# Reordering the start of a hybrid pool and state-space block: a tile's squares ahead of the step sizes, their exponential in two pieces, and one set of transposes ahead of the first product

## The chip, the cores and the metric

The kernel runs on one core of a Trainium2 chip. The metric is device time in microseconds (us) of one execution; lower is better. The core's engines each work through a stream of instructions of their own, in order, and wait for one another through semaphores: TensorE (PE, with its weight loads as PEld), VectorE (DVE), ScalarE (ACT), GpSimd (POOL), and SyncE (SP), which here only issues DMAs.

## The reference, cut to what matters

One decoder layer on x of 1024 tokens by 1024 channels, float32. What the change touches is the front of it:

```python
mod = jax.nn.silu(c) @ w_ada + b_ada
shift, scale, gate = jnp.split(mod, 3, axis=-1)
h = rmsnorm(x, norm_pre) * (1.0 + scale[:, None, :]) + shift[:, None, :]
proj = h @ w_in            # 6144 columns: u_pool, z_pool, u_ssm, z_ssm, g_pool, g_ssm
...
dt = jnp.exp(log_dt)[:, None]          # step sizes of the states
abar = exp(lam * dt)                   # used by the state-space mixer much later
```

`rmsnorm(x, gain)` is `x * rsqrt(mean(x*x) + 1e-6) * gain`, per token. Behind it come two mixers, gates and three more square products, and the output `x + gate * rmsnorm(out, norm_post)`.

## The kernel before, in words

Every engine's order is written out by hand; there is no scheduler. All products are split in three: an operand is written as a high part and a low part (`split_hi` or `h_high` on ScalarE, `split_lo` or `split_h` on VectorE), and TensorE adds high by high, high by low and low by high.

x is read as eight tiles of 128 tokens (`x_tok`), in order, with the constants (which hold the identity) between tiles 2 and 3. The sum of squares of each tile goes to one of two engines (`X_TILES_ACT`, `X_TILES_DVE`): ScalarE squares tiles 0, 1, 3 for the first half and 4, 6, 7 for the second, VectorE tile 2 and tile 5 (`square_sum`, L1404). For each half VectorE waits for all four sums, forms the variance (L1417), ScalarE takes the root (L1032), VectorE makes the reciprocal (`newton`) and four diagonal matrices (`diag`, L1422). TensorE multiplies 128 by 128 blocks of x by such a diagonal (`transposed(k, tiles)`, L1976), which transposes and normalises them at once. K tiles 0 to 3 are done half by half, in the order 2, 0, 1, 3 (`XT_ORDER`); K tiles 4 to 7 afterwards, whole. Only four PSUM areas hold them, so a transposed tile must be copied out before its area is written again: `xt_out(k)` on ScalarE copies K tile k to `h_full` and counts `xt_taken`. `transposed(4)` waits for one such copy, that of K tile 2; `transposed(5)` for two, so for K tile 3 as well, whose area it takes. K tiles 0 and 1 have no copy of their own: `h_of(0)` and `h_of(1)` read them in PSUM.

The modulation: ScalarE applies SiLU to c, and for each K tile k VectorE sums rows of `w_ada` against it (`scale_sum`, `shift_sum`, L1400) to give one column each of `g_col` and `s_col` (L1436, L1438). `h_of(k)` on ScalarE (L1051) then makes K tile k of h, `h_high(k)` (L1057) its high part and `split_h(k)` on VectorE (L1442) its low part, which counts `h_done`. In VectorE's order `split_h(0)` stands between `scale_sum(1)` and `shift_sum(1)`, and `split_h(1)` behind `shift_sum(2)`.

TensorE runs the first two products (`gs` 0 and 1) side by side, one K tile of each in turn: `step(n, k)` waits for `h_done` above k. `step(1, 0)` also waits for `h_of(1)`, whose PSUM area it takes, and for the low part of its weights. The third product is fitted in as K tiles come; from the fourth on whole products follow.

On VectorE the step sizes of the states come first of all: `plain_angles` computes `dt = exp(log_dt)` and two multiples of the angle on 128 by 64 values, a chain of small instructions, each of which waits for the one before. Their result is next read after the last `split_h`, by `reduced_angles`.

Of the kernel before, what the change touches and what calls it, by code (L numbers as in the profile page):

```python
# [36 lines left out]
CH = 8  # L37
NC = SEQ // CH
HALF = 512
G = 64  # L40
# [83 lines left out]
def previous(p):  # L124

    if p == 4:
        return JOB[USES[0]]
    q = p - 2
    while q >= 0 and USES[q][0] == "ga":
        q -= 2  # L130
    return None if q < 0 else JOB[USES[q]]


def half_pi_parts():

    unit = 10 ** 35
    rest, parts = 157079632679489661923132169163975144, []
    rest <<= 34
    for bits in (10, 22, 34):
        n = rest // (unit << (34 - bits))  # L140
        parts.append(n / 2 ** bits)
        rest -= n * (unit << (34 - bits))
    return parts + [rest / (unit << 34)]


class Steps:
# [13 lines left out]
    def do(self, ins):  # L160
        self.did(ins)
        self.landed()


def build(nc, x, c_d, cols_d, consts_d, a_re_d, a_im_d, log_dt_d, bc_d, w_ada_d, wstream_d, pool_d, w_out_d, out):
    ctx = ExitStack()
    with ctx:
        def sem(name):
            return ctx.enter_context(nc.semaphore(name))
# [44 lines left out]
        def hb(q, k):  # L214

            return bop[:, 2 * (k // 4):2 * (k // 4) + 2, q, k % 4, :]

        def halves(ap):

            return ap.rearrange("p (f m) -> p f m", f=2)  # L220
# [171 lines left out]
        v_sums, par_in, xt_taken = sem("v_sums"), sem("par_in"), sem("xt_taken")  # L392
# [54 lines left out]
        def slot(u):  # L447

            return SLOT[JOB[u]]
# [21 lines left out]
        par = {}  # L471
# [5 lines left out]
        wide = {}  # L477
# [47 lines left out]
        def rounded(steps, out_, in_, scale):  # L525

            steps.do(nc.vector.tensor_scalar(out_, in_, scale, MAGIC, ALU.mult, ALU.add))
            steps.do(nc.vector.tensor_scalar(out_, out_, MAGIC, None, ALU.subtract))

        def exp(steps, out_, in_, width):  # L530

            do = steps.do
            tt, stt, ts = nc.vector.tensor_tensor, nc.vector.scalar_tensor_tensor, nc.vector.tensor_scalar
            k, r, p, q = (wide[z][:, 0:width] for z in ("k", "r", "p", "q"))
            do(ts(q, in_, -87.0, 88.0, ALU.max, ALU.min))
            rounded(steps, k, q, 1.4426950408889634)
            do(stt(r, k, -0.693359375, q, ALU.mult, ALU.add))
            do(stt(r, k, 2.12194440054690583e-4, r, ALU.mult, ALU.add))
            c = [1.0, 1 / 2, 1 / 6, 1 / 24, 1 / 120, 1 / 720]
            do(ts(p, r, 1 / 5040, None, ALU.mult))  # L540
            for a in reversed(c):
                do(stt(p, p, a, r, ALU.add, ALU.mult))
            do(ts(p, p, 1.0, None, ALU.add))
            do(ts(bits[:, 0:width], k, 127.0, 8388608.0, ALU.add, ALU.mult))
            do(tt(p, p, bits[:, 0:width].bitcast(F32), ALU.mult))
            do(stt(out_, in_, -87.0, p, ALU.is_ge, ALU.mult))

        def plain_angles(steps):

            do, tt, ts = steps.do, nc.vector.tensor_tensor, nc.vector.tensor_scalar  # L550
            exp(steps, par["dt"], par["ldt"], G)
            do(tt(wide["ang"][:, 0:G], par["aim"], par["dt"], ALU.mult))
            do(ts(wide["ang"][:, G:], wide["ang"][:, 0:G], float(CH), None, ALU.mult))

# [9 lines left out]
        def reduced_angles(steps):  # L564

            do, stt = steps.do, nc.vector.scalar_tensor_tensor
            k, r, q = (wide[m] for m in ("k", "r", "q"))
            src = wide["ang"]
            for scale in (2048.0, 1.0):
                rounded(steps, k, src, 1.0 / (1.5707963267948966 * scale))  # L570
                for part in half_pi_parts():
                    do(stt(r, k, -part * scale, src, ALU.mult, ALU.add))
                    src = r
            rounded(steps, q, k, 0.25)
            do(stt(q, q, -4.0, k, ALU.mult, ALU.add))
# [430 lines left out]
        def _(act):  # L1006
            fn = nc.scalar.activation

            def split_hi(p):

                act.wait_ge(raw_in[p % 2], 16 * (p // 2) + 16)
                if p != 2 and previous(p) is not None:
                    act.wait_ge(mm_done, previous(p) + 1)
                fn((wx_hi if p == 2 else w_hi[p % 2])[:, :, :], raw[p % 2][:, :, :], ACT.Copy).then_inc(hi_done, 1)  # L1014
# [22 lines left out]
            def xt_out(k):  # L1037

                act.wait_ge(xt_done, XT_ORDER.index(k) + 1)
                fn(h_full[k][:, :], xt[k][:, :], ACT.Copy).then_inc(xt_taken, 1)  # L1040
# [13 lines left out]
            def h_high(k):  # L1054

                act.wait_ge(h_ready, k + 1)
                fn(hb(0, k), halves(h_full[k][:, :]), ACT.Copy).then_inc(h_hi_done, 1)  # L1057

            split_hi(0)
            xt_out(2)  # L1060
            h_of(0)
            h_high(0)
            xt_out(3)
            split_hi(1)
            h_of(1)
            xt_out(4)
# [319 lines left out]
        def _(dve):  # L1386
            tt, stt = nc.vector.tensor_tensor, nc.vector.scalar_tensor_tensor
            ts = nc.vector.tensor_scalar
            steps = Steps(dve, dve_step)
            do, did = steps.do, steps.did  # L1390

            def split_lo(p):

                dve.wait_ge(hi_done, SPLIT[USES[p]] + 1)
                hi, lo = (wx_hi, wx_lo) if p == 2 else (w_hi[p % 2], w_lo[p % 2])
                tt(lo[:, :, :], raw[p % 2][:, :, :], hi[:, :, :].bitcast(F32), ALU.subtract).then_inc(raw_free[p % 2], 1)  # L1396
# [5 lines left out]
            def square_sum(t):  # L1402
                dve.wait_ge(tile_in[t], 16)
                stt(rt[1][:, :], x_tok[:, t, :], 1.0, x_tok[:, t, :], ALU.mult, ALU.mult,  # L1404
                    accum_out=stat[:, 0, t:t + 1]).then_inc(v_sums, 1)

            dve.wait_ge(par_in, 16 * 3)
            plain_angles(steps)
            for half_ in range(2):
                cols4 = slice(4 * half_, 4 * half_ + 4)  # L1410
                for t in X_TILES_DVE[half_]:
                    if half_:
                        dve.wait_ge(v_sums, half_)
                    square_sum(t)
                dve.wait_ge(v_sums, half_ + 1)
                dve.wait_ge(x_sums, 3 * half_ + 3)
                ts(stat[:, 1, cols4], stat[:, 0, cols4], 1.0 / D, EPS, ALU.mult, ALU.add).then_inc(x_var, 1)  # L1417
                dve.wait_ge(x_root, half_ + 1)
                newton(steps, cols4, 1.0)
                dve.wait_ge(small_in, 16)  # L1420
                for t in range(4 * half_, 4 * half_ + 4):
                    ts(diag[:, t, :], ident, stat[:, 4, t:t + 1], None, ALU.mult).then_inc(x_scaled, 1)  # L1422
                if half_ == 0:
                    dve.wait_ge(cols_in, 16)
                    do(ts(g_col[:, :], b_ada[:, KT:2 * KT], 1.0, None, ALU.add))
# [14 lines left out]
            def split_h(k):  # L1440
                dve.wait_ge(h_hi_done, k + 1)
                tt(hb(1, k), halves(h_full[k][:, :]), hb(0, k).bitcast(F32), ALU.subtract).then_inc(h_done, 1)  # L1442

            dve.wait_ge(silu_ready, 1)
            for k in range(KT):
# [8 lines left out]
                if k == 3:  # L1454
                    split_lo(2)
            split_h(KT - 1)
            reduced_angles(steps)
            sine(steps)
            split_lo(3)
# [445 lines left out]
            for t in range(CH):  # L1905
# [3 lines left out]
                bank, g, r = ps[slot(u)], gt[t % 2], rt[t % 2]  # L1909
# [24 lines left out]
        def _(pe):  # L1934
# [34 lines left out]
            def transposed(k, tiles):  # L1969

                if k >= 4:
                    pe.wait_ge(xt_taken, 5 if k == 7 else k - 3)
                for t in tiles:
                    if k == XT_ORDER[0]:
                        pe.wait_ge(x_scaled, t + 1)
                    last = mm(xt[k][:, t * P:t * P + P], x_tok[:, t, k * P:k * P + P], diag[:, t, :],  # L1976
                              start=True, stop=True)
                if CH - 1 in tiles:
                    last.then_inc(xt_done, 1)

            def step(n, k):

                u = ("gs", n)
                if k == 0:
                    begin(u)
                    if n == 1:
                        pe.wait_ge(h_ready, 2)
                    elif n == 2:
                        pe.wait_ge(xt_taken, 4)
                pe.wait_ge(h_done, k + 1)  # L1990
                last = k_step(u, k, *h)
                if k == KT - 1:
                    last.then_inc(mm_done, 1)

            for tiles in (range(0, 4), range(4, CH)):
                for k in XT_ORDER[:4]:
                    transposed(k, tiles)
            transposed(4, range(CH))
            step(0, 0)
            transposed(5, range(CH))  # L2000
            step(1, 0)
            third = {2: (0, 1), 3: (2,), 5: (3,), 7: (4, 5, 6, 7)}
            for k in range(1, KT):
# [278 lines left out]
```

## Time and profile before

| what | value |
|---|---|
| time, median of 3 runs | 953.89 us (953.86 to 953.91) |
| profiled execution, first to last instruction (span) | 951.7 us |
| PE busy | 930.3 us, 98% of the span |
| DVE busy | 640.0 us, 67% |
| ACT busy | 347.6 us, 37% |
| mean granted TensorE clock | 0.999 of full speed |

The profiled execution's own time stands nowhere apart from the three runs; its span lies 2.2 us below their median, which is what lies around the first and last instruction. PE busy counts matmuls whose ends are modelled, so a busy PE is not PE at its peak. Idle time is worth something only where the chain that ends last passes through it.

### The profile page before, as it was taken

The numbers are of one execution on the slowest core, as the hardware profiler recorded it, in microseconds if no ns is written. First come the engines' busy times: TensorE is split into PE (matmuls) and PEld (weight loads), VectorE is DVE, ScalarE is ACT, GpSimd is POOL, SyncE is SP. The second block draws the span as 40 slices with busy tenths as digits, with TensorE's granted clock in tenths as the row PEclk, the third lists the DMA queues.
The fourth block names the chain that finished last, engine by engine and source line by source line (L and its number), as shares of the span: only waits on it lengthen the run. The fifth ranks groups of instructions, "written<-read, shape, count | busy, mean of one in ns | idle before, by whom it ended". The sixth has DMA issues, their size and how long they took to land.

```text
span 951.7 us, 11609 instructions
## 1 busy us (share of the span) xinstructions
PE 930.3 (98%) x4408; PEld 781.6 (82%) x4408; DVE 640.0 (67%) x916; ACT 347.6 (37%) x453; POOL 45.4 (5%) x82
## 2 busy tenths in 40 slices
PE   4999999999999999999999999999999999999997
PEld 4888888888888888888888888888888888888885
DVE  5988999877788887437898789665344444455232
ACT  6741353334444444434444436441022221223111
POOL 0019700000000000000000000000000000000000
PEclk9999999999999999999999999999999999999999
DMA  9843355446555444556898582597643268422222
GB/s 352 299 153 125 124 200 166 156 159 195 174 188 202 147 176 152 191 131 183 228 245 224 132 205 88 165 339 262 182 161 107 89 228 202 144 89 89 89 88 89
DMA packets 95719, 164.60 MB, mean 173 GB/s; under 512 B 38576, under 2 KB 55088, under 8 KB 95664
## 3 DMA queue, kind: packets, MB, share of 16 engines
q1 hardware_dynamic: 85872, 159.31, 52.1%
q10 hardware_dynamic: 9792, 4.56, 1.9%
q8 instruction: 35, 0.57, 0.3%
q14 instruction: 20, 0.16, 0.1%
HBM read 116.64 MB, written 47.19 MB: 172 GB/s over the span
## 4 chain that ended last, share of the span: by engine, by line
PE 97%; DVE 1%; ACT 1%; DMA 1%; issue 0%; ACTq 0%; DVEq 0%
PE ps L1948 49%; PE ps L2068 20%; PE ps L2190 9%; PE psb L2068 8%; PE ps L2139 2%; PE psb L2119 2%; PE psb L2128 2%; PE psa L2107 2%; PE psa L2026 1%; PE psa L1948 1%; DMA par_are<-in_a_re 1%; PE psb L2026 0%; PE psb L1976 0%; ACT gt L1028 0%; DVE mod_out L1400 0%
## 5 line engine op out<-in xcount | busy, mean ns | idle before, releaser
L1948 PE MATMUL ps<-bop,w_hi 128*128 128x512 f32 x1120 | 300.6, 390 | 0.9 <-DVE bop L1442 0.9
L1948 PEld LDWEIGHTS ps<-bop,w_hi 128*128 128x128 f32 x1120 | 209.3, 188 | 44.0 <-issue 1.1
L1948 PE MATMUL ps<-bop,w_lo 128*128 128x512 f32 x560 | 172.3, 389 | 0.0
L1948 PEld LDWEIGHTS ps<-bop,w_lo 128*128 128x128 f32 x560 | 105.1, 188 | 21.8
L1396 DVE TENSOR_TENSOR w_lo<-raw,w_hi 128x1024 fp32r<-128x1024 f32 x43 | 53.3, 1239 | 46.9 <-ACT w_hi L1014 46.7
L2068 PE MATMUL ps<-bop,r_hi 128*128 128x512 f32 x272 | 83.7, 389 | 0.0
L1014 ACT ACTIVATE w_hi<-raw 128x1024 fp32r<-128x1024 f32 x43 | 45.3, 1053 | 68.7 <-PE ps L1948 56.3
L2068 PEld LDWEIGHTS ps<-bop,r_hi 128*128 128x128 f32 x272 | 51.1, 188 | 10.6
L2068 PE MATMUL ps<-t_hi,r_hi 128*128 128x512 f32 x140 | 55.1, 393 | 0.0
L2068 PE MATMUL ps<-t_hi,r_lo 128*128 128x512 f32 x140 | 54.5, 390 | 0.0
L2068 PE MATMUL ps<-t_lo,r_hi 128*128 128x512 f32 x140 | 54.5, 389 | 0.0
L2068 PE MATMUL ps<-bop,r_lo 128*128 128x512 f32 x136 | 52.9, 389 | 0.0
L2190 PE MATMUL ps<-wo_hi,y_hi 128*128 128x512 f32 x128 | 49.8, 389 | 0.0
L2190 PE MATMUL ps<-wo_lo,y_hi 128*128 128x512 f32 x128 | 49.8, 389 | 0.0
L2190 PE MATMUL ps<-wo_hi,y_lo 128*128 128x512 f32 x128 | 49.8, 389 | 0.0
L1627 DVE TENSOR_TENSOR r_lo<-r_f,r_hi 128x512 fp32r<-128x512 f32 x56 | 37.2, 687 | 10.2 <-ACT r_hi L1129 10.2
L1869 DVE SCALAR_TENSOR_TENSOR y_raw<-gt,y_raw 128x1024 f32<-128x1024 f32 x8 | 9.8, 1226 | 47.9 <-ACT gt L1084 47.9
L1948 PE MATMUL ps<-y_hi,w_hi 128*128 128x512 f32 x128 | 39.4, 389 | 0.0
L1948 PE MATMUL ps<-y_lo,w_hi 128*128 128x512 f32 x128 | 39.4, 389 | 0.0
L1948 PE MATMUL ps<-y_hi,w_lo 128*128 128x512 f32 x128 | 39.4, 389 | 0.0
L1129 ACT ACTIVATE r_hi<-r_f 128x512 fp32r<-128x512 f32 x56 | 32.3, 624 | 17.9 <-DVE r_f L1607 14.3
L1914 DVE TENSOR_SCALAR stat<-stat 128x1 f32<-128x1 f32 x7 | 1.1, 154 | 49.3 <-ACT squares L1375 49.3
(318 smaller groups left out, 1575.4 us busy)
## 6 DMA issues: line engine op xcount, KB each, us to landing
raw<-in_wstream SPq DMA_DIRECT2D x52, 512.0 KB, 5.1
pair_raw<-in_wstream SPq DMA_DIRECT2D x26, 512.0 KB, 4.2
ada<-in_w_ada SPq DMA_DIRECT2D x16, 512.0 KB, 11.2
x_tok<-in_x SPq DMA_DIRECT2D x8, 512.0 KB, 6.8
gs_d<-gt SPq DMA_DIRECT2D x8, 512.0 KB, 5.1
win_d<-win_new SPq DMA_DIRECT2D x8, 512.0 KB, 2.7
wout_d<-wout_new SPq DMA_DIRECT2D x8, 512.0 KB, 3.8
wout<-wout_d SPq DMA_DIRECT2D x8, 512.0 KB, 4.7
```

What stands on the lines that cost most here:

```text
L1014: fn((wx_hi if p == 2 else w_hi[p % 2])[:, :, :], raw[p % 2][:, :, :], ACT.Copy).then_inc(hi_done, 1)
L1129: fn(r_hi[o // 4][:, o % 4, :].rearrange("p (k m) -> p k m", m=P), src, ACT.Copy).then_inc(pair_hi, 1)
L1396: tt(lo[:, :, :], raw[p % 2][:, :, :], hi[:, :, :].bitcast(F32), ALU.subtract).then_inc(raw_free[p % 2], 1)
L1627: tt(lo, full, hi.bitcast(F32), ALU.subtract).then_inc(pair_lo, 1)
L1869: stt(y_raw[:, n, :], gt[n % 2][:, :], 1.0, y_raw[:, n, :], ALU.add, ALU.mult).then_inc(gated, 1)
L1948: last = mm(ps[slot(u)][:, f * HALF:f * HALF + HALF], a[:, k, :], b(k, f), start=k == order[0] and q == 0, stop=k == order[-1] and q == 2)
L2068: last = mm(bank, a, b, start=k == 0 and q == 0 and not adds, stop=k == 3 and q == 2, skip_group_check=adds)
L2107: last = mm(psa[:, g * P:g * P + P], win[:, g, :], u_in[m % 2][:, g, :], start=True, stop=True)
L2119: last = mm(psb[:, g * P:g * P + P], taps[:, g, :, :].rearrange("p r h -> p (r h)"), u_in[m % 2][:, g, :], start=g % 4 == 0, stop=True, sk ...
L2128: last = mm(psb[:, g * P:g * P + P], wout[:, g, :, :].rearrange("p r h -> p (r h)"), sq[:, g, :], start=False, stop=True, skip_group_check ...
L2139: last = mm(ps[slot(u)][:, f * HALF:f * HALF + HALF], a[:, 2 * q + k, :], b[:, k, f * HALF:f * HALF + HALF], start=k == 0 and p == 0, stop ...
L2190: ins = mm(ps[slot(("out", t))][:, f * HALF:f * HALF + HALF], a[:, k, t * P:t * P + P], b[:, f * HALF:f * HALF + HALF], start=first and q ...
```

## The change

Four orders are rewritten; no instruction is added or taken away.

1. VectorE starts with `square_sum(2)`, without waiting for the step sizes' inputs. `exp` is cut in two: `exp_front` (five instructions) stands behind `square_sum(2)` and ahead of the first variance; `exp_back` (eleven) behind `square_sum(5)` and ahead of the second variance.
2. What remains of `plain_angles` (two instructions) moves behind the last `split_h`, ahead of `reduced_angles`.
3. ScalarE copies K tile 2 ahead of the first weight split, and K tile 3 ahead of `h_of(0)` and `h_high(0)`, where it stood behind both.
4. TensorE does `transposed(5)` ahead of `step(0, 0)` and no longer behind it.

```diff
-        def exp(steps, out_, in_, width):
+        def exp_front(steps, in_, width):
             do(ts(q, in_, -87.0, 88.0, ALU.max, ALU.min))
             rounded(steps, k, q, 1.4426950408889634)
             do(stt(r, k, -0.693359375, q, ALU.mult, ALU.add))
             do(stt(r, k, 2.12194440054690583e-4, r, ALU.mult, ALU.add))
+        def exp_back(steps, out_, in_, width):
             c = [1.0, 1 / 2, 1 / 6, 1 / 24, 1 / 120, 1 / 720]
             do(ts(p, r, 1 / 5040, None, ALU.mult))
             for a in reversed(c):
...
+        def exp(steps, out_, in_, width):
+            exp_front(steps, in_, width)
+            exp_back(steps, out_, in_, width)
+
         def plain_angles(steps):
-            exp(steps, par["dt"], par["ldt"], G)
             do(tt(wide["ang"][:, 0:G], par["aim"], par["dt"], ALU.mult))
             do(ts(wide["ang"][:, G:], wide["ang"][:, 0:G], float(CH), None, ALU.mult))
...
+            xt_out(2)
             split_hi(0)
-            xt_out(2)
+            xt_out(3)
             h_of(0)
             h_high(0)
-            xt_out(3)
             split_hi(1)
             h_of(1)
             xt_out(4)
...
-            dve.wait_ge(par_in, 16 * 3)
-            plain_angles(steps)
             for half_ in range(2):
                 cols4 = slice(4 * half_, 4 * half_ + 4)
                 for t in X_TILES_DVE[half_]:
                     if half_:
                         dve.wait_ge(v_sums, half_)
                     square_sum(t)
+                dve.wait_ge(par_in, 16 * 3)
+                if half_ == 0:
+                    exp_front(steps, par["ldt"], G)
+                else:
+                    exp_back(steps, par["dt"], par["ldt"], G)
                 dve.wait_ge(v_sums, half_ + 1)
                 dve.wait_ge(x_sums, 3 * half_ + 3)
                 ts(stat[:, 1, cols4], stat[:, 0, cols4], 1.0 / D, EPS, ...).then_inc(x_var, 1)
...
             split_h(KT - 1)
+            plain_angles(steps)
             reduced_angles(steps)
...
             transposed(4, range(CH))
+            transposed(5, range(CH))
             step(0, 0)
-            transposed(5, range(CH))
             step(1, 0)
```

## Rows read from the trace of the kernel before

**Rows 1.** The page's chain that ended last, its shares of the span by engine.

```profile
PE 97%; DVE 1%; ACT 1%; DMA 1%; issue 0%; ACTq 0%; DVEq 0%
```

**Rows 2.** All waits of PE: releaser, us in total, times, longest us.

```profile
PE psb L1976 <- DVE diag L1422: 14.3, 1, 14.3
PE ps L1948 <- DVE bop L1442: 0.9, 1, 0.9
```

**Rows 3.** Timeline, PE: start us, duration us, instructions, [idle before, releaser].

```profile
14.27 2.08 PE L1976 MATMUL psb<-diag,x_tok 128*128 128x128 f32 x8 [14.27 <-DVE diag L1422]
...
19.56 1.06 PE L1976 MATMUL psb<-diag,x_tok 128*128 128x128 f32 x8
...
23.13 1.95 PE L1976 MATMUL psb<-diag,x_tok 128*128 128x128 f32 x16
26.03 1.15 PE L1948 MATMUL ps<-bop,w_hi 128*128 128x512 f32 x4 [0.95 <-DVE bop L1442]
...
29.17 1.17 PE L1948 MATMUL ps<-bop,w_hi 128*128 128x512 f32 x4
...
32.33 1.17 PE L1948 MATMUL ps<-bop,w_hi 128*128 128x512 f32 x4
...
64.15 1.07 PE L1948 MATMUL ps<-bop,w_hi 128*128 128x512 f32 x4
```

**Rows 4.** Timeline, DVE, same columns.

```profile
6.96 0.20 DVE L535 TENSOR_SCALAR par_w_q<-par_ldt 128x64 f32<-128x64 f32 x1 [6.96 <-DMA par_are<-in_a_re]
...
8.16 0.20 DVE L540 TENSOR_SCALAR par_w_p<-par_w_r 128x64 f32<-128x64 f32 x1
...
10.93 0.22 DVE L552 TENSOR_TENSOR par_w_ang<-par_aim,par_dt 128x64 f32<-128x64 f32 x1
...
11.42 1.22 DVE L1404 SCALAR_TENSOR_TENSOR rt<-x_tok 128x1024 f32<-128x1024 f32 x1
...
12.69 0.17 DVE L1417 TENSOR_SCALAR stat<-stat 128x4 f32<-128x4 f32 x1
...
13.93 0.87 DVE L1422 TENSOR_SCALAR diag<-consts,stat 128x128 f32<-128x128 f32 x4
...
14.92 1.23 DVE L1404 SCALAR_TENSOR_TENSOR rt<-x_tok 128x1024 f32<-128x1024 f32 x1
...
16.72 0.17 DVE L1417 TENSOR_SCALAR stat<-stat 128x4 f32<-128x4 f32 x1 [0.57 <-ACT gt L1028]
...
19.53 1.23 DVE L1400 SCALAR_TENSOR_TENSOR mod_out<-ada,silu_row 128x1024 f32<-128x1024 f32 x1 [0.69 <-ACT silu_row L1034]
...
22.08 0.15 DVE L1438 TENSOR_TENSOR s_col<-mod_acc,cols 128x1 f32<-128x1 f32 x1
...
24.66 1.23 DVE L1442 TENSOR_TENSOR bop<-h_full,bop 128x1024 fp32r<-128x1024 f32 x1
...
27.20 0.15 DVE L1438 TENSOR_TENSOR s_col<-mod_acc,cols 128x1 f32<-128x1 f32 x1
...
31.02 1.22 DVE L1442 TENSOR_TENSOR bop<-h_full,bop 128x1024 fp32r<-128x1024 f32 x1
...
60.98 1.23 DVE L1396 TENSOR_TENSOR w_lo<-raw,w_hi 128x1024 fp32r<-128x1024 f32 x1
```

**Rows 5.** Timeline, ACT, same columns.

```profile
10.65 0.19 ACT L1028 ACTIVATION_READ_ACCUMULATOR gt<-x_tok 128x1 f32 x1
...
21.21 1.01 ACT L1040 ACTIVATE h_full<-psb 128x1024 f32<-128x1024 f32 x1
22.33 1.20 ACT L1051 ACTIVATE h_full<-ps,s_col,g_col 128x1024 f32<-128x1024 f32 x1
...
27.45 1.20 ACT L1051 ACTIVATE h_full<-ps,s_col,g_col 128x1024 f32<-128x1024 f32 x1 [0.96 <-DVE s_col L1438]
```

**Rows 6.** DMA issues running at 2.1 and 5.6 us (tiles 2, 7): size, us to landing.

```profile
x_tok<-in_x SPq DMA_DIRECT2D x1, 512.0 KB, 6.0
...
x_tok<-in_x SPq DMA_DIRECT2D x1, 512.0 KB, 9.4
```

More of the change, by code:

```diff
@@ L528, in rounded @@
             steps.do(nc.vector.tensor_scalar(out_, out_, MAGIC, None, ALU.subtract))
-        def exp(steps, out_, in_, width):
+        def exp_front(steps, in_, width):
             do = steps.do
-            tt, stt, ts = nc.vector.tensor_tensor, nc.vector.scalar_tensor_tensor, nc.vector.tensor_scalar
+            stt, ts = nc.vector.scalar_tensor_tensor, nc.vector.tensor_scalar
             k, r, p, q = (wide[z][:, 0:width] for z in ("k", "r", "p", "q"))
@@ L538, in exp @@
             do(stt(r, k, 2.12194440054690583e-4, r, ALU.mult, ALU.add))
+        def exp_back(steps, out_, in_, width):
+            do = steps.do
+            tt, stt, ts = nc.vector.tensor_tensor, nc.vector.scalar_tensor_tensor, nc.vector.tensor_scalar
+            k, r, p = (wide[z][:, 0:width] for z in ("k", "r", "p"))
             c = [1.0, 1 / 2, 1 / 6, 1 / 24, 1 / 120, 1 / 720]
```

## The prediction

> **What bounds the kernel now.** I read the chain of waits first: 97% of the span is TensorE [rows 1]. Then TensorE's own waits over the whole span: only two [rows 2], 14.3 us until the first diagonal matrices are there, and 0.9 us ahead of the first product. After 26 us TensorE never waits again that the profile shows. So the time is TensorE's work plus those two, and the change is worth what it does to the moment from which TensorE no longer waits. Third, I read the timelines of TensorE, VectorE and ScalarE from 6 to 33 us side by side [rows 3 to 5], to find which event lets each step start.
>
> The reader is to see one thing there that the list of waits hides. The 0.95 us ahead of the first product, `step(0, 0)` at 26.03 [rows 3], looks like time to be filled, and the new order on TensorE fills it with `transposed(5)`. But `step(0, 1)` at 32.33 needs `split_h(1)`, which runs on VectorE from 31.02 for 1.22 and so ends at 32.24 [rows 3, 4]. TensorE arrives there 0.1 us after VectorE is done: no wait is shown, yet there is hardly any slack. And VectorE's row of instructions from `split_h(0)` at 24.66 to 31.02 lists no idle time. So `split_h(0)` sets when `step(0, 1)` can start, and what TensorE does earlier changes nothing there. From then on TensorE has the same work to do with or without the change. The question is: when does `split_h(0)` start?
>
> **The change, part by part.** All times on the span's clock.
>
> *First half, VectorE and ScalarE.* Tile 2 lands at about 2.1 + 6.0 = 8.1 [rows 6]. Its square takes 12.69 - 11.42 = 1.27 [rows 4], so until 9.4. `exp_front` takes 8.16 - 6.96 = 1.20 [rows 4], so until 10.6. ScalarE's third sum, bound by its tile, ends at 10.65 + 0.19 = 10.84 [rows 5], so `exp_front` is hidden, with 0.2 to spare. With 0.1 for the hand-over (as from 27.20 + 0.15 on VectorE to 27.45 on ScalarE [rows 4, 5]) the first variance is at 10.94, 1.75 earlier than 12.69. Diagonals follow 13.93 - 12.69 = 1.24 later, TensorE 0.34 behind these [rows 3, 4]: it starts at 12.52 in place of 14.27.
>
> *Second half, VectorE.* From the first variance to `square_sum(5)` it is 14.92 - 12.69 = 2.23 [rows 4], so that starts at 13.17 and ends at 14.44. Now stands `exp_back`: 10.93 - 8.16 = 2.77 [rows 4]. The second variance comes at 17.21; before it was at 16.72, when ScalarE's sixth sum released it [rows 4]. So it is 0.49 late, and with it the roots, SiLU and the sums of the modulation. The second piece does not fit in VectorE's wait there, as worked out under the rivals.
>
> *TensorE's transposes.* The first 32 took 19.56 - 14.27 = 5.29, the second 32 23.13 - 19.56 = 3.57 [rows 3]. Starting at 12.52, the first are done at 17.81. The second diagonals come at 17.21 + 1.24 = 18.45 and TensorE starts on them at 18.8: a new idle of 1.0 us. It gives them out at 0.2 us each at first, so the last transpose of K tile 3 ends at 22.5. Of the 1.75 us gained in front, some 0.8 are left here (18.8 against 19.56).
>
> *ScalarE.* Now `xt_out(3)` stands ahead of `h_of(0)`. It waits for those last transposes of K tile 3, at 22.5, and takes 1.0 like the copy at 21.21 [rows 5]. Behind it in ScalarE's queue stand `h_of(0)`, `h_high(0)`, the second weight split and `h_of(1)`. `h_of(0)` thus starts at 23.4 (an instruction of ScalarE starts some 0.1 ahead of the modelled end of the last), where it stood at 22.33 [rows 5]: 1.08 late. The modulation, 22.08 + 0.15 + 0.49 = 22.72 [rows 4], does not bind. `split_hi(0)` now follows the copy of K tile 2, which the earlier transposes let start at 20.0, and so ends at about 22.0; its low part on VectorE, behind the sums, starts after 22.6, so this costs nothing.
>
> *VectorE.* From `h_of(0)` to `split_h(0)` it is 24.66 - 22.33 = 2.33 [rows 4, 5], so `split_h(0)` starts at 25.74, 1.08 late. VectorE is free from 25.0 (its sums 0.49 late), so 0.7 us of it is a new wait, and `shift_sum(1)`, `split_lo(1)`, the sums of K tile 2 and `split_h(1)`, queued behind, all move by 1.08.
>
> *TensorE, products.* `transposed(4)` and `transposed(5)` take 3.57/2 = 1.79 each behind the second half and end at about 26.0; both copies they need are there (21.0 and 23.5). `step(0, 0)` follows `split_h(0)` by 26.03 - 24.66 = 1.37 [rows 3, 4]: 27.11, after an idle of 1.1. `step(1, 0)` needs `h_of(1)`: its column is there at 27.35 + 1.08 = 28.43, the instruction runs from 28.53 for 1.20 [rows 5], so TensorE starts at 29.8 (29.17 before), having waited 1.3. With 32.33 - 29.17 = 3.16 for this step and `transposed(6)` it would be at `step(0, 1)` at 33.0. `split_h(1)` now starts at 31.02 + 1.08 = 32.10, and by 1.31 to 1.37 behind it [rows 3, 4] the step starts at 33.4 to 33.5, 1.1 later than 32.33.
>
> *The rest of the exponential.* The two instructions behind the last `split_h` take 11.42 - 10.93 = 0.49 [rows 4] and push VectorE's later work back. Next late is `split_lo(3)`: it ended at 60.98 + 1.23 = 62.21 and its product began at 64.15 [rows 3, 4], 1.9 of cover, more than 0.49. GpSimd's table and the store of its coefficients also start 0.49 later beside TensorE; if a step of TensorE waited for that with no slack, 0.49 would be its price. No wait of TensorE is on the list there, so I take 0.
>
> *DMAs.* None is added. SyncE's third weight load waits for `split_lo(0)`, 0.49 later, and the later rows of `w_ada` queue behind it. VectorE's sums show no wait for a DMA in the rows [rows 4], and they are themselves 1.08 later. I take 0; at worst 0.49, less what that delay covers, so nothing.
>
> **Sum.** TensorE reaches its unbroken stretch 1.1 later (1.08 to 1.14). 951.7 + 1.1 = 952.8 for the span; the median lies 2.2 above the span, so 955.0, 0.12% slower. For this forecast alone the range is 954.4 to 955.6: downward to half the delay if ScalarE's hand-overs overlap better, upward by the 0.49 above.
>
> **A rule against the trace.** The first eight matmuls start over 1.87 us, 0.23 each; eight of the second half over 0.9, 0.11 each [rows 3]: half speed (1.2 GHz) after a start from idle, then full (2.4 GHz). After the 0.95 us idle at 25.08 the spacing stays at full speed: four 512 column matmuls span 1.15, as the 1.17 at 29.17 without an idle ahead [rows 3]. The Trainium skill ("TensorE: Matmul & The Clock Gate", Part 1) says that the half rate is the default state, that activity releases it, and that idling brings it back. By that rule the new idles, 1.0, 1.1, 1.3 and 0.4 us within fifteen, are a danger that the sum leaves out; by the row after 25.08 they are none. I take the row.
>
> **Rivals.**
>
> *The clock falls.* If TensorE drops to 1.2 GHz in one of the idles ahead of `step(0, 0)` or `step(1, 0)`, it pays once more what it paid at its start: 5.29 - 3.57 = 1.7 [rows 3]. Against it: the idle at 25.08, alone. For it: here two longer ones lie 1.4 us apart. 955.0 + 1.7 = 956.7.
>
> *The pieces fit, and it gets faster.* The place is VectorE's wait between `square_sum(5)` and the second variance. Tile 7 lands at 5.4 + 9.4 = 14.8 [rows 6]; ScalarE's square of it and hand-over end at 16.05. The room is 16.05 - 14.44 = 1.6 us; `exp_back` needs 2.77. If it ran in 1.6 or less, the variance would be 0.67 earlier, `h_of(0)` would still stand behind `xt_out(3)`, and the first half's transposes would end the second at 21.4, so `h_of(0)` at 22.4, as before: 953.9. Only if ScalarE's copy were also no hindrance would `split_h(0)` move up, by 0.67 and the 0.14 that VectorE waited there: 953.1, not faster by 0.2%.
>
> *Nothing is seen.* TensorE has `transposed(5)` behind it at `step(0, 0)`, 1.7 us of work. If `split_h(1)` were not what `step(0, 1)` needs in time, that work would pay for the later start and the end would stay: 953.9. Against it stand 32.24 and 32.33.
>
> **How the numbers follow.** A delay of 1.1 us: 0.70, at 955.0. Clock: 0.11, 956.7. Nothing seen: 0.08, 953.9. Faster: 0.06, 953.1. Something late behind VectorE's 0.49, with more than one place: 0.05, 955.5 to 956.5. The range that leaves out no more than 2 in 10 reaches from 954.0 to 956.8. About 0.2%, 1.9 us, is what a measurement can tell from no change: 952.0 to 955.8 is "same". That holds the forecast, nothing seen and nearly all of faster: 0.81. Slower is the clock and a part of the last: 0.16. Faster by more than 1.9 would need more than both gains together: 0.03.
>
> **What would show it.** Right, if the first transposes start near 12.5, the second variance at 17.2, K tile 3's copy at 22.5 ahead of `h_of(0)` at 23.4, `split_h(0)` at 25.7 behind a wait for ScalarE, and TensorE's list of waits has four new entries with `step(0, 1)` at 33.4. Wrong, if the second variance follows ScalarE, if `h_of(0)` stands at or before 22.4, if `step(0, 1)` starts before 32.6, or if matmuls behind an idle are spaced at half speed.

## The result, and the profile after

The changed kernel took 955.01 us (median of 21 runs, 954.63 to 955.64), the kernel before 953.58 beside it (21 runs, 953.13 to 954.65). The ratio is 1.0014, 95% interval 1.0008 to 1.0020: 1.43 us or 0.14% slower. The interval leaves out 1, so the difference is clear of the noise, but it is smaller than the 0.2% up to which the prediction speaks of "same". The profiled execution has a span of 953.7 and a time of its own of 955.46. In it x landed later than in the execution profiled before: ScalarE's first square starts at 5.73, there at 5.43. I put these 0.30 down to the execution and not to the change (in the profiles of the experiments the same instruction starts between 5.18 and 5.77, at 5.18 in e3 and at 5.77 in e7), so in what follows I take them off wherever I say "less 0.30", and likewise the offset of each experiment.

The page of the changed kernel, the chain that ended last, by engine:

```profile
PE 93%; DVE 4%; ACT 1%; DMA 1%; issue 1%; SPq 0%; DVEq 0%; ACTq 0%
```

All waits of TensorE (releaser, us in total, times, longest us):

```profile
PE psb L1990 <- DVE diag L1435: 13.8, 2, 12.9
PE ps L1962 <- DVE w_lo L1406: 1.1, 1, 1.1
PE ps L1962 <- DVE bop L1455: 1.1, 1, 1.1
PE ps L2082 <- ACT gt L1148: 0.3, 1, 0.3
```

Where before two waits stood [rows 2], there are five. The longest is 1.4 shorter than it was (12.9 for 14.3), but 0.93, 1.07, 1.09 and 0.26 have come or stayed behind it (the first of these four is the second wait in the first line). The timeline shows where (start, duration, instructions, idle before them):

```profile
12.88 2.07 PE L1990 MATMUL psb<-diag,x_tok 128*128 128x128 f32 x8 [12.88 <-DVE diag L1435]
...
19.02 1.16 PE L1990 MATMUL psb<-diag,x_tok 128*128 128x128 f32 x8 [0.93 <-DVE diag L1435]
...
24.48 1.95 PE L1990 MATMUL psa<-diag,x_tok 128*128 128x128 f32 x16
27.51 1.17 PE L1962 MATMUL ps<-bop,w_hi 128*128 128x512 f32 x4 [1.07 <-DVE bop L1455]
...
30.23 1.17 PE L1962 MATMUL ps<-bop,w_hi 128*128 128x512 f32 x4 [1.09 <-DVE w_lo L1406]
...
33.77 0.50 PE L1962 MATMUL ps<-bop,w_hi 128*128 128x512 f32 x1
...
136.78 0.47 PE L2082 MATMUL ps<-t_hi,r_hi 128*128 128x512 f32 x1 [0.26 <-ACT gt L1148]
```

TensorE starts 1.39 earlier than in [rows 3], at 19.02 it has 0.54 of that left, and at `step(0, 1)` it is 1.44 late (33.77 against 32.33), of which 0.30 is x's landing. VectorE and ScalarE, same view:

```profile
11.30 0.17 DVE L1430 TENSOR_SCALAR stat<-stat 128x4 f32<-128x4 f32 x1 [0.55 <-ACT gt L1038]
...
17.18 0.22 DVE L552 SCALAR_TENSOR_TENSOR par_dt<-par_ldt,par_w_p 128x64 f32<-128x64 f32 x1
17.43 0.17 DVE L1430 TENSOR_SCALAR stat<-stat 128x4 f32<-128x4 f32 x1
...
26.14 1.22 DVE L1455 TENSOR_TENSOR bop<-h_full,bop 128x1024 fp32r<-128x1024 f32 x1 [0.91 <-ACT bop L1067]
...
32.49 1.22 DVE L1455 TENSOR_TENSOR bop<-h_full,bop 128x1024 fp32r<-128x1024 f32 x1
```

```profile
22.89 1.03 ACT L1050 ACTIVATE h_full<-psa 128x1024 f32<-128x1024 f32 x1 [0.71 <-PE psa L1990]
23.82 1.20 ACT L1061 ACTIVATE h_full<-ps,s_col,g_col 128x1024 f32<-128x1024 f32 x1
25.05 1.06 ACT L1067 ACTIVATE bop<-h_full 128x1024 fp32r<-128x1024 f32 x1
```

The first variance follows ScalarE and has 0.55 to spare, so `exp_front` is hidden. The second, at 17.43, has no idle time ahead of it: it follows `par_dt`, the last instruction of `exp_back`. On ScalarE the copy of K tile 3 waits 0.71 for TensorE, `h_of(0)` stands right behind it, and so VectorE waits 0.91 for `h_high(0)` ahead of `split_h(0)`.

Then TensorE runs 1.44 to 1.49 behind its trace of before up to the sixth half product, and 1.79 to 1.83 from there to 502 us (136.78, where it was 134.95). TensorE waits there for a copy of ScalarE at 136.06. Upstream of it an instruction of VectorE, `t_lo`, lasts longer than before (GpSimd's and VectorE's timeline of the changed kernel):

```profile
116.51 1.07 POOL L514 TENSOR_TENSOR coef<-tmp_c,tmp_d 128x256 f32<-128x256 f32 x1
116.91 2.81 DVE L1503 TENSOR_TENSOR t_lo<-t_f,t_hi 128x2048 fp32r<-128x2048 f32 x1
```

The same instructions before, and TensorE's first matmul of the sixth half product:

```profile
114.09 1.06 POOL L514 TENSOR_TENSOR coef<-tmp_c,tmp_d 128x256 f32<-128x256 f32 x1
115.62 2.28 DVE L1489 TENSOR_TENSOR t_lo<-t_f,t_hi 128x2048 fp32r<-128x2048 f32 x1
134.95 0.47 PE L2068 MATMUL ps<-t_hi,r_hi 128*128 128x512 f32 x1
```

There `t_lo` began when GpSimd's last instruction was done. Now that instruction, which hangs on the moved angles, is later and the two overlap. From 504.74 us on TensorE is 1.9 to 2.0 behind: there the weight load of `taps` waits 0.15 for its DMA, which it did not before. That small wait differs between the profiles and has no cause in the rows.

### The profile page after: what moved, and what is told of

It is laid out like the page before. It is cut to its first block, busy times and chain, and to the rows that moved or that the text cites. A ratio compares the mean times of both kernels' runs of the same rounds, so it can differ in the third digit from the quotient of the medians.

```text
span 953.7 us, 11608 instructions
## 1 busy us (share of the span) xinstructions
PE 931.1 (98%) x4408; PEld 781.4 (82%) x4408; DVE 639.8 (67%) x916; ACT 347.6 (36%) x453; POOL 45.8 (5%) x82
## 4 chain that ended last, share of the span: by engine, by line
PE 93%; DVE 4%; ACT 1%; DMA 1%; issue 1%; SPq 0%; DVEq 0%; ACTq 0%
PE ps L1962 47%; PE ps L2082 19%; PE ps L2204 9%; PE psb L2082 8%; PE ps L2153 2%; PE psb L2133 2%; PE psb L2142 1%; PE psa L2121 1%; PE psa L2040 1%; PE psa L1962 1%; DVE t_lo L1503 1%; DMA x_tok<-in_x 1%; PE psb L2040 0%; DVE mod_out L1410 0%; PE psb L1990 0%
## 5 line engine op out<-in xcount | busy, mean ns | idle before, releaser
L1139 ACT ACTIVATE r_hi<-r_f 128x512 fp32r<-128x512 f32 x56 | 32.3, 625 | 17.9 <-DVE r_f L1621 14.3
```

The lines of the kernel that those rows point to most:

```text
L1139: fn(r_hi[o // 4][:, o % 4, :].rearrange("p (k m) -> p k m", m=P), src, ACT.Copy).then_inc(pair_hi, 1)
```

## Experiments

Each time stands against runs of the kernel before on the same chip beside it: 953.71 us for e1 to e4, 954.18 for e5 to e7, 953.76 for e8 and e9.

| label | edit | us | difference | ratio, 95% interval |
|---|---|---|---|---|
| e1_act_order | changed kernel, ScalarE's old order | 954.31 | +0.60 | 1.0005, 0.9996 to 1.0014 |
| e2_exp_first | changed kernel, VectorE's old order | 955.66 | +1.95 | 1.0022, 1.0012 to 1.0031 |
| e3_pe_only | kernel before, TensorE's edit alone | 953.32 | -0.39 | 0.9998, 0.9989 to 1.0007 |
| e4_angles_early | changed kernel, angles ahead of the sums | 954.53 | +0.82 | 1.0010, 1.0001 to 1.0019 |
| e5_fitted | exponential in three pieces, both other orders old | 954.45 | +0.27 | 1.0003, 0.9994 to 1.0012 |
| e6_fitted_copy_first | the same pieces, both other orders new | 954.77 | +0.59 | 1.0007, 0.9998 to 1.0016 |
| e7_vector_only | kernel before, VectorE's edit alone | 955.11 | +0.93 | 1.0009, 1.0000 to 1.0018 |
| e8_fitted_filled | e5 with TensorE kept at work | 953.41 | -0.35 | 0.9997, 0.9987 to 1.0006 |
| e9_pe_undone | changed kernel, TensorE's old order | 956.43 | +2.67 | 1.0027, 1.0016 to 1.0038 |

The difference is that of the medians; the ratio is not that of the medians, so the two can differ in the last digit. The times alone tell few of these from one another; what decides is each profile.

**e1_act_order** puts ScalarE's old order back: K tile 2's copy behind the first weight split, K tile 3's behind `h_of(0)` and `h_high(0)`.

```diff
-            xt_out(2)
             split_hi(0)
-            xt_out(3)
+            xt_out(2)
             h_of(0)
             h_high(0)
+            xt_out(3)
```

> The changed kernel with ScalarE's old order (K tile 3 copied behind h_of(0) and h_high(0)). Theory (h_of(0) is held up by xt_out(3), and the second piece of the exponential makes the rest 0.49 late): h_of(0) starts 0.5 later than in the kernel before (22.8 on its clock) instead of 1.1, split_h(0) at 25.2, step(0, 1) at 32.8, and with some 0.35 of the wait at the pair products 0.8 us slower than before, 0.6 faster than the changed kernel. Rival (ScalarE's order is hidden, the exponential alone makes the loss): 1.4 slower than before, as the changed kernel. Rival (transposes that wait for the late copy hold TensorE): step(0, 0) only at 27.8, and the loss stays over 1.4.

Its timelines of ScalarE, VectorE and TensorE, and a line of TensorE's waits:

```profile
22.92 1.20 ACT L1061 ACTIVATE h_full<-ps,s_col,g_col 128x1024 f32<-128x1024 f32 x1 [0.46 <-DVE s_col L1451]
...
25.24 1.23 DVE L1455 TENSOR_TENSOR bop<-h_full,bop 128x1024 fp32r<-128x1024 f32 x1
...
32.88 1.20 PE L1962 MATMUL ps<-bop,w_hi 128*128 128x512 f32 x4
```

```profile
PE psa L1990 <- ACT h_full L1050: 1.6, 1, 1.6
```

`h_of(0)` no longer follows a copy but the modulation, and `step(0, 1)` is at 32.88, less 0.18 (first square at 5.61) 0.37 late in place of 1.14. So the copy's place is 0.77 of the front, and the second variance's delay the rest. The wait for the copy has gone to `transposed(5)`, 1.6 us, and costs nothing there: as the second rival said, `step(0, 0)` starts only at 27.8 (27.98 less 0.18), but `step(0, 1)` is not held by it, and the loss did not stay over 1.4. `t_lo` took 2.82 in this profile too, and TensorE again waited 0.3 at the sixth half product: 0.37 and 0.35 make 0.72 where 0.60 was measured.

**e2_exp_first** does the whole of `plain_angles` at VectorE's start again.

```diff
+            dve.wait_ge(par_in, 16 * 3)
+            exp(steps, par["dt"], par["ldt"], G)
+            plain_angles(steps)
             for half_ in range(2):
...
-                dve.wait_ge(par_in, 16 * 3)
-                if half_ == 0:
-                    exp_front(steps, par["ldt"], G)
-                else:
-                    exp_back(steps, par["dt"], par["ldt"], G)
```

> The changed kernel with VectorE's old order (whole exponential and angles first), ScalarE's and TensorE's new. Theory (xt_out(3) waits for the end of the transposes, and h_of(0) for it): the second variance is back at 16.7, yet the transposes end at 23.3, so h_of(0) starts at 24.2, split_h(0) at 26.6, step(0, 1) at 34.2: 1.9 us slower than before and some 0.5 slower than the changed kernel; no wait at the pair products. Rival (the exponential ahead of the second variance makes the loss): as the kernel before, 0.0.

The expected +1.9 came as +1.95. Without the earlier start of the transposes the new place of the copy costs more, since K tile 3's transposes are later: `h_of(0)` stands right behind the copy here too. In this profile one more thing is seen, TensorE's first transposes:

```profile
14.34 2.08 PE L1987 MATMUL psb<-diag,x_tok 128*128 128x128 f32 x8 [14.34 <-DVE diag L1433]
16.20 3.62 PE L1987 MATMUL ps<-diag,x_tok 128*128 128x128 f32 x16
19.62 1.48 PE L1987 MATMUL psa<-diag,x_tok 128*128 128x128 f32 x8
20.93 1.06 PE L1987 MATMUL psb<-diag,x_tok 128*128 128x128 f32 x8
```

The first 32 matmuls take 6.59 us, for the same work 5.29 in [rows 3]: the slow start lasted longer (the second row's 16 matmuls start over 3.42 us, 0.21 each, where those from 20.93 on start 0.11 apart). The granted clock reads 1.00 in every window of this stretch, so that the slow start is TensorE's clock is taken from the spacing alone. This profiled execution took 956.67, 1.0 above the median. Where the transposes are on the path, as here, a longer slow start moves the end; that a shorter one makes the median's +1.95 is inferred, since no execution near the median was profiled.

**e3_pe_only** does `transposed(5)` ahead of `step(0, 0)` in the kernel before.

```diff
             transposed(4, range(CH))
+            transposed(5, range(CH))
             step(0, 0)
-            transposed(5, range(CH))
```

> The kernel before with TensorE's edit alone: transposed(5) ahead of step(0, 0). Theory (step(0, 1) hangs on split_h(1), so the idle ahead of step(0, 0) is worth nothing): transposed(5) waits for K tile 3's copy until 25.5, step(0, 0) starts at 27.3, step(1, 0) at 28.8, step(0, 1) at 32.3 to 32.4; 0.0 to 0.1 slower than before. Rival (the filled idle is a gain): 0.4 to 0.95 faster than before.

TensorE's timeline at `step(0, 1)`:

```profile
32.12 1.20 PE L1948 MATMUL ps<-bop,w_hi 128*128 128x512 f32 x4
```

The idle ahead of the first product is gone from TensorE's list, which keeps only the wait for the first diagonals (14.1). `step(0, 0)` moves back to 27.23, and `step(0, 1)` stands at 32.12; with an offset of -0.25 that is 0.04 later than in [rows 3], not earlier. The interval of the time holds 1. Filling that idle alone is worth nothing that these runs can tell.

**e4_angles_early** moves the two remaining instructions of `plain_angles` to VectorE's wait for SiLU.

```diff
+            plain_angles(steps)
             dve.wait_ge(silu_ready, 1)
...
             split_h(KT - 1)
-            plain_angles(steps)
             reduced_angles(steps)
```

> The changed kernel with the two remaining instructions of the angles put ahead of VectorE's wait for SiLU, where it idles 0.7, instead of behind the last split_h. Theory (these 0.49 push GpSimd's table past the end of its overlap with VectorE's t_low, which costs TensorE some 0.35 at the sixth half product): the front as in the changed kernel, TensorE's wait for ScalarE's copy of the first half product gone, 1.0 to 1.1 slower than before, 0.35 faster than the changed kernel. Rival (that wait comes from the late front alone): 1.4 slower than before, as the changed kernel.

The list of waits and the two instructions of the overlap:

```profile
PE psb L1990 <- DVE diag L1435: 13.3, 2, 12.4
PE ps L1962 <- DVE bop L1455: 1.2, 2, 1.1
PE ps L1962 <- DVE w_lo L1406: 1.1, 1, 1.1
```

```profile
115.05 1.06 POOL L514 TENSOR_TENSOR coef<-tmp_c,tmp_d 128x256 f32<-128x256 f32 x1
...
116.59 2.28 DVE L1503 TENSOR_TENSOR t_lo<-t_f,t_hi 128x2048 fp32r<-128x2048 f32 x1
```

The wait for `gt` is gone, `t_lo` is back at 2.28, and the shift at the sixth half product (135.93 against 134.95) is the 0.97 to 0.98 that it was at `step(0, 1)`, with x landing 0.14 early. So what was added at 136.78 came with the moved angles. That the overlap with GpSimd is what lengthens `t_lo` rests on the profiles side by side: 2.81 and 2.82 in the two where GpSimd's last instruction is still under way (the changed kernel and e1), 2.28 in the nine others, where it was done 0.47 to 0.48 before `t_lo` began. Two of these nine, e7 and e9, have the moved angles too. So the move alone does not bring the overlap; in those two profiles TensorE was later still (`step(0, 1)` at 34.32 and 35.11 without the offsets, 33.47 in the changed kernel), and VectorE waits 0.83 for ScalarE at 63 us, where it does not wait in the changed kernel.

**e5_fitted** cuts the exponential in three, so that each piece fits: five instructions ahead of `square_sum(2)`, five behind it, six behind `square_sum(5)`. The angles stand as in e4, `h_of(0)` ahead of `xt_out(3)`, TensorE's order is the old one.

```diff
+            dve.wait_ge(par_in, 16 * 3)
+            exp_front(steps, par["ldt"], G)
             for half_ in range(2):
...
-                dve.wait_ge(par_in, 16 * 3)
                 if half_ == 0:
-                    exp_front(steps, par["ldt"], G)
+                    exp_mid(steps, G)
                 else:
-                    exp_back(steps, par["dt"], par["ldt"], G)
+                    exp_end(steps, par["dt"], par["ldt"], G)
...
             xt_out(2)
             split_hi(0)
-            xt_out(3)
             h_of(0)
             h_high(0)
+            xt_out(3)
```

> The exponential in three pieces that fit VectorE's waits (five instructions ahead of square_sum(2), where VectorE idles until 8.1; five behind it; six behind square_sum(5)), the angles ahead of the wait for SiLU, ScalarE's copy of K tile 2 ahead of the first weight split, K tile 3's copy and TensorE's order as before. Theory (the end follows split_h(0), which follows the second variance once nothing else holds h_of(0)): the second variance follows ScalarE's sixth sum at 16.05, h_of(0) at 21.7, VectorE then waits for w_ada's second K tile until 22.9, split_h(0) at 24.1, step(0, 1) at 31.8: 0.5 us faster than before, no wait at the pair products. Rival (the front is bound elsewhere, the squares are not worth anything): 0.0.

Lines of VectorE's timeline:

```profile
15.99 0.17 DVE L1440 TENSOR_SCALAR stat<-stat 128x4 f32<-128x4 f32 x1 [0.28 <-ACT gt L1047]
...
23.98 1.23 DVE L1465 TENSOR_TENSOR bop<-h_full,bop 128x1024 fp32r<-128x1024 f32 x1
```

The pieces fit: the second variance is at 15.99, released by ScalarE, and `split_h(0)` at 23.98, 0.68 earlier than in [rows 4] (0.55 without the offset of -0.13). Yet `step(0, 1)` is at 33.29. TensorE's timeline from 25 us:

```profile
25.35 1.24 PE L1972 MATMUL ps<-bop,w_hi 128*128 128x512 f32 x4 [2.00 <-DVE bop L1465]
...
27.24 3.12 PE L2000 MATMUL psa<-diag,x_tok 128*128 128x128 f32 x16
...
30.12 1.17 PE L1972 MATMUL ps<-bop,w_hi 128*128 128x512 f32 x4
```

Windows of 2 us (busy time of PE, PEld, DVE, ACT, POOL with counts, granted clock, DMA share, GB/s):

```profile
26.00:28.00 2.00, 2.00 (x9) 1.69 (x8) 1.96 (x6) 1.23 (x2) 0.00 (x0) 0.57 1.03 397
28.00:30.00 2.00, 2.00 (x13) 2.00 (x13) 2.00 (x3) 1.83 (x2) 0.00 (x0) 0.57 1.05 384
```

TensorE, with its transposes done early, now idles 2.0 us in one piece ahead of `step(0, 0)`. In the work behind it the granted clock is 0.57 over four microseconds (in windows of half a microsecond it reads 1.00 until 26.0, 0.50 from 26.5 to 29.5 and 1.00 from 30.0; 0.50 is 1.2 GHz of 2.4), and `step(0, 0)` with `transposed(5)` takes 4.77 where it took 3.14 [rows 3]: 1.6 lost, more than was gained. It seems not to happen in each execution: the four of its eleven timed runs with a mean clock of 0.997 took 954.20 to 955.12, the two at 0.998 954.67 and 954.94, the five at 0.999 953.11 to 954.60, four of these under 953.9. A wait of 0.5 for `taps` at 504 us in this and the next profile stays unexplained; it adds to both times.

**e6_fitted_copy_first** is e5 with the change's orders on ScalarE and TensorE.

```diff
             split_hi(0)
+            xt_out(3)
             h_of(0)
             h_high(0)
-            xt_out(3)
...
             transposed(4, range(CH))
-            step(0, 0)
             transposed(5, range(CH))
+            step(0, 0)
```

> The same pieces of the exponential with ScalarE's and TensorE's order of the changed kernel (K tile 3's copy ahead of h_of(0), transposed(5) ahead of step(0, 0)). Theory (the copy waits for the end of TensorE's transposes, which now follow one another without a wait and so carry the time that TensorE's clock takes to rise, 14 to 28 matmuls at half speed in the executions seen): transposes end at 21.4 to 22.5, h_of(0) at 22.3 to 23.4, split_h(0) at 24.7 to 25.7: 0.0 to 1.0 slower than before, some 0.5 to 1.4 faster than the changed kernel, and its runs spread over more than those of the three pieces with the old copy. Rival (the copy's place is hidden): as the three pieces with the old copy, 0.5 faster than before.

Its timelines of ScalarE and VectorE:

```profile
21.66 1.02 ACT L1059 ACTIVATE h_full<-psa 128x1024 f32<-128x1024 f32 x1 [0.62 <-PE psa L2000]
22.59 1.20 ACT L1070 ACTIVATE h_full<-ps,s_col,g_col 128x1024 f32<-128x1024 f32 x1
...
24.91 1.22 DVE L1465 TENSOR_TENSOR bop<-h_full,bop 128x1024 fp32r<-128x1024 f32 x1 [0.97 <-ACT bop L1076]
```

The copy starts at the very 21.66 at which `h_of(0)` starts in e5: its place costs 0.93, nearly one copy's time, even where the second variance is on time. TensorE's idles are 1.1 and 1.1, and the clock stays at 1.00.

**e7_vector_only** does VectorE's edit in the kernel before (in the changed kernel, e1's and e9's diffs together).

> The kernel before with VectorE's edits alone (exponential in two pieces, angles behind the last split_h). Theory: the second variance 0.49 late, h_of(0) and split_h(0) 0.49 late, step(0, 1) at 32.8, and 0.35 more at the sixth half product: 0.8 us slower than before, the same as the kernel that lacks only ScalarE's edit. Rival (VectorE's edits are hidden, the loss is all ScalarE's): 0.0.

With an offset of +0.34, `split_h(0)` at 25.36 is 0.36 late, much as in e1 (0.40), but TensorE has nothing left to do ahead of `step(0, 0)` and idles 2.07 us (its timeline, and a window of 2 us):

```profile
26.73 1.41 PE L1962 MATMUL ps<-bop,w_hi 128*128 128x512 f32 x4 [2.07 <-DVE bop L1455]
```

```profile
28.00:30.00 2.00, 2.00 (x9) 1.81 (x8) 2.00 (x3) 1.85 (x2) 0.00 (x0) 0.50 0.99 339
```

In the profiled execution (956.01) the clock fell behind that idle, and `step(0, 0)` with `transposed(5)` took 4.77 again. Its four runs at a mean clock of 0.997 took 955.11 to 956.07, its five at 0.999 took 953.93 to 954.77: the median of +0.93 is a mixture of the two, so that it agrees with the expected +0.8 is no proof of it. Of that 0.8, the 0.35 at the sixth half product is not in this profile: less the 0.34 `step(0, 1)` is 1.99 late (34.66) and the sixth half product 1.96 (137.25).

**e8_fitted_filled** is e5 with K tile 4's transposes done twice, the first time for nothing, to keep TensorE at work in the idle.

```diff
+            pe.wait_ge(xt_taken, 1)
+            for t in range(CH):
+                mm(xt[4][:, t * P:t * P + P], x_tok[:, t, 4 * P:5 * P], diag[:, t, :], start=True, stop=True)
             transposed(4, range(CH))
             step(0, 0)
```

> The three pieces with the old copy (which showed an idle of 2.0 us on TensorE ahead of step(0, 0), and behind it TensorE's granted clock at 0.57), with the transposes of K tile 4 done twice over, so that TensorE works through 1.8 of those 2.0. The first pass is redundant work. Theory (the idle lets the clock fall, and that ate the 0.7 that VectorE's earlier split_h(0) gives): no matmul behind 17 us spaced at half speed, step(0, 0) still at 25.3, step(0, 1) at 31.7, 0.5 to 0.7 faster than the kernel before but for a wait of up to 0.6 on the taps' DMA at 504 us, and 0.5 to 1 faster than the same without the filling. Rival (the clock falls for another reason, or the filling delays the first product): 0.0 to 0.5 slower than before, as the three pieces without it.

All of TensorE's waits, and lines of its windows and timeline:

```profile
PE psb L2000 <- DVE diag L1445: 12.4, 1, 12.4
```

```profile
26.00:28.00 2.00, 2.00 (x15) 1.78 (x14) 1.96 (x6) 1.24 (x2) 0.00 (x0) 1.00 1.01 391
28.00:30.00 2.00, 2.00 (x15) 1.79 (x14) 2.00 (x3) 2.00 (x3) 0.00 (x0) 1.00 1.05 386
```

```profile
31.87 1.17 PE L1972 MATMUL ps<-bop,w_hi 128*128 128x512 f32 x4
```

With work that computes nothing in that place, the clock stays at 1.00, no run has a mean clock under 0.998, and `step(0, 1)` is at 31.87, 1.42 earlier than in e5's profile. The span is 951.1, the shortest of the study. Against the kernel before it is at -0.35 where e5 was at +0.27; this profile also lacks the wait for `taps`, so not all of the difference between the two need be the clock. Its interval holds 1, and e3 is as low at -0.39: it is 1.8 below the changed kernel (-0.35 and +1.43), and not measurably below the kernel before.

**e9_pe_undone** takes TensorE's edit out of the changed kernel.

```diff
             transposed(4, range(CH))
-            transposed(5, range(CH))
             step(0, 0)
+            transposed(5, range(CH))
             step(1, 0)
```

> The changed kernel without TensorE's edit: transposed(5) again behind step(0, 0). TensorE then idles in one piece, from 24.1 to 27.1 on the clock of the prediction. Theory (an idle of that length lets the clock fall, two of 1.1 do not): the first products and transposed(5) run at half speed for some 3 us, 1.6 more; step(0, 1) at 35, 955.0 + 1.6 = 956.6 in the executions where it falls, 3 us slower than before. Rival (only VectorE's chain counts, the clock stays): as the changed kernel, 1.4 slower than before.

TensorE's wait, and its windows:

```profile
PE ps L1962 <- DVE bop L1455: 2.9, 1, 2.9
```

```profile
28.00:30.00 2.00, 2.00 (x8) 1.69 (x7) 1.97 (x6) 1.34 (x2) 0.00 (x0) 0.54 1.03 381
30.00:32.00 2.00, 2.00 (x13) 2.00 (x13) 1.99 (x4) 1.73 (x2) 0.00 (x0) 0.60 1.04 337
```

`split_h(0)` and `split_h(1)` stand as in the changed kernel (25.87 and 32.23, less 0.06; there 26.14 and 32.49, less 0.30). But the idle of 2.86 is in one piece, the clock falls to 0.54, and `step(0, 0)` with `transposed(5)` takes 4.77 (27.24 to 32.01). Five of its seven runs have a mean clock of 0.997, one of 0.998; the one at 0.999 is the fastest, 955.22, near the changed kernel. Against the kernel before, it is 1.2 slower than with the edit (+2.67 and +1.43).

## Why the prediction was right, point by point

**First half.** Right. The first variance is at 11.30, less 0.30 11.00 (forecast 10.94), the transposes start at 12.58 (12.52).

**Second half.** Right. The second variance is at 17.43, less 0.30 17.13 (17.21), behind VectorE's own work and not ScalarE's; TensorE idles 0.93 (1.0) and, with 0.30 taken off, starts on it at 18.72 (18.8).

**The copy ahead of `h_of(0)`.** Right, and the main cause: with 0.30 taken off the copy starts at 22.59 (22.5), `h_of(0)` at 23.52 (23.4), `split_h(0)` at 25.84 (25.74). e1 takes the copy away and 0.77 of the 1.14 with it. e6 against e5 shows a like price, 0.93, without the late variance.

**The products.** Right in the times: with 0.30 taken off the three steps start at 27.21, 29.93 and 33.47 (27.11, 29.8, 33.4 to 33.5), the last 1.14 late. Of the four new waits the fourth, 0.4 ahead of `step(0, 1)`, is not on the list: the modelled end of `transposed(6)`, 33.64, covers most of it. The wait ahead of `step(1, 0)` came as 1.09 for 1.3, and the list names the low part of the weights as its releaser, not `h_of(1)`; `split_lo(1)` ends at 29.97 and `h_of(1)` at 30.13, so the two are close, and which of them set the start is not settled.

**The rest of the exponential: mis-sized.** I took 0 with a bound of 0.49, since no wait of TensorE was listed there. It cost 0.35. The place I checked, `split_lo(3)`, was not the one; it was GpSimd's table, which I named and dismissed. Its last instruction came to lie over `t_lo` on VectorE, and ScalarE's copy behind it was late by 0.3 for TensorE. `t_lo` began 0.67 before GpSimd's row ends and took 0.53 longer. The Trainium skill ("SBUF — State Buffer", Who interferes with whom) says that a VectorE instruction with two SBUF inputs contends with a GpSimd instruction that reads SBUF. The trace agrees in kind with these 0.53. So the bound of 0.49 held, but it was sized as a plain delay; what came was a collision, and e7 and e9, with the same move, show none.

**The total.** 955.0 against 955.01 is better than the sum deserves. The base was 0.31 too high (953.89 from three runs, 953.58 from 21), and the missing 0.35 made up for it: 953.58 + 1.14 + 0.35 = 955.07. The 2.2 from span to time has the same error in it: in each timed run of the changed kernel, and in each run of the experiments and of the kernel before beside them, span and time are 1.7 to 1.9 apart, so 2.2 was not what lies around the first and last instruction. With 1.8 the profile of before stands for 953.5. The chances have a slip too: the 0.81 for "same" counts only half of "faster", not nearly all of it.

**The rivals.** "Nothing is seen" fell with `step(0, 1)`; e3 shows that filling the idle is worth nothing by itself. "The pieces fit" is not this kernel, whose second variance follows `exp_back`; e5 shows that pieces of another size do fit, and that faster still doesn't follow. "The clock falls" did not happen here (1.00 in every 2 us window from 24 to 34 us, no run of the 21 with a mean clock under 0.998), but it is real and near, and I had weighed it by the wrong thing. Its price was nearly right, 1.7 for 1.6 (4.77 against 3.14), though I had it from the slow start, where the granted clock reads 1.00 and half speed is read from the spacing alone. I counted short idles close together. What the runs show is single idles: behind 0.93, 1.07 and 1.09 (changed kernel) and 1.61 (e1) the clock stayed, behind 2.00 (e5), 2.07 (e7) and 2.86 (e9) it was 0.50 to 0.60 over windows of 2 us, by the mean clocks in a part of the executions. e8 against e5 and the changed kernel against e9 show that filling or splitting the idle keeps the clock; that its length alone decides is not shown, since runs of one kernel differ. TensorE's edit, which I thought worthless, is what cuts the changed kernel's idle in two; it is worth the 1.2 between e9 and the changed kernel. Between 1.61 and 2.00 nothing was tried. The Trainium skill ("TensorE: Matmul & The Clock Gate", Part 1) says that idling brings the half rate back, and that the number of slow matmuls at a kernel's start varies from run to run. The 0.50 in the three profiles agrees with the first, and the starts of 5.29 and 6.59 us with the second; that the fall behind an idle varies too is what the mixed runs of e5, e7 and e9 indicate.

**What stays open.** The runs of the kernel before spread over 1.5 us, and no profile here shows why. The length of the slow start varies between the profiles by up to 1.3 us (e2 against [rows 3]) without a cause in the rows. So differences of a few tenths between medians, as of e3 and e8 from the kernel before, are not explained by anything here.

## What to carry to other kernels

An idle on the busiest engine is worth what lies behind it: follow it to the point where that engine no longer waits, and see which other engine's row sets that point. A copy moved ahead in an in-order queue hands its own lateness to everything behind it, so ask when its input comes, not when its consumer wants it. Where a rearrangement gathers TensorE's idle time into one stretch of 2 us or more, look at the granted clock behind it; splitting the idle, or filling it even with work that computes nothing, kept the clock here.

## What the hardware showed that I had not expected

- Behind an idle of 2.00 to 2.86 us TensorE's granted clock stayed at 1.00 for the first 0.7 to 1.0 us of work, then fell to 0.50 (1.2 GHz) for more than 3 us, and a step of 3.14 us took 4.77; by the mean clocks not in every execution of the same kernel.
- The same 32 matmuls of the first transposes took 5.29 us in one execution [rows 3] and 6.59 in another (e2), at a granted clock that reads 1.00 in both.
- A subtraction of 128 by 2048 values on VectorE took 2.81 and 2.82 us with a GpSimd instruction still under way (two profiles) and 2.28 without (nine).
